# Two-block transformer stack on one core: at every norm the scaling of the rows goes ahead of the next weight splits on VectorE, and a bank wait on TensorE is narrowed

## The chip, the cores and the metric

The kernel runs on one core of a Trainium2 chip. The metric is the device time of one execution in microseconds. Line numbers are those of the kernel before.

## The reference

The input is one sequence of 256 rows of 1024 numbers in float32. Two parts follow one another. The first has two layers; each is a mixer (an mLSTM in layer 0, stick-breaking attention in layer 1), a cross-attention into 256 memory rows and a gated feed-forward of width 2816. Ahead of each stage the rows go through a root-mean-square norm, and what a stage gives is normed again and added:

```python
x = x + rms_norm(y, g[1])
y = memory_cross_attention(rms_norm(x, g[2]), mem_n, xa_w_q[layer], xa_w_kv[layer], xa_w_o[layer])
x = x + rms_norm(y, g[3])
y = swiglu_ffn(rms_norm(x, g[4]), ffn_w_gate_up[layer], ffn_w_down[layer])
x = x + rms_norm(y, g[5])
```

The second part has one layer: three mixers side by side (a gated recurrence, a forgetting attention, a memory attention), gated and merged, then a feed-forward with a short convolution. In all there are eight norms of the rows `xr` whose result goes into products, numbered 0 to 7.

## The kernel before, in words

Five engines run a program each and meet at semaphores. Each engine serves its own instructions in order, so the order in which a program is written decides what stands behind what.

**Weights.** All weights are streamed. They are cut into chunks in a fixed list (`order`), of which each has one or, mostly, two pieces of 128x1024 numbers. SyncE loads the chunks into `raw` (three buffers); it waits until the low halves of the chunk three back are made. Products are made in three terms so that they keep nearly float32 precision: each piece is split into a high half `whi`, which ScalarE makes (L989), and a low half `wlo = raw - whi`, which VectorE makes (L1468). Both have four buffers (`NSP`), and ScalarE waits for TensorE to have used the piece four back (`w_used`). `past(name)` on either engine makes all halves up to four pieces beyond the chunk `name`.

**Products.** `fm` (L373 to L375) multiplies a chunk piece by piece with the weights as the stationary operand, `tm` (L393 to L395) with the rows as the stationary operand, first both pieces for tile 0 (128 rows), then for tile 1. TensorE waits for each piece's low half (`w_lo`), and so for both its halves.

**A norm.** After a stage's last product ScalarE squares its result (`post_squares`, L1037), GpSimd makes the reciprocal root (`rstd`, L2034 and L2035), VectorE scales it and adds it to `xr` (`post_add`, L1516 and L1520); this is per tile. Then the next norm begins: ScalarE squares `xr` (`squares`, L1007), GpSimd makes the root, VectorE scales the rows (`normed`, L1488, semaphore `n_x`), TensorE transposes them (`norm_rows`, L418, 16 transposes), ScalarE makes the high half of each of the eight transposed rows blocks (`norm_hi`, L1021), VectorE the low half (`norm_lo`, L1498, semaphore `n_lo`), and products begin. At norm 7 `post_squares` is missing and the addition is a single instruction (`plain_add`, L1526).

TensorE has other work between a stage's last product and the transposes. At norm 1 these are the chunks K0_3 and V0_1a, at norm 2 K1_0 and K1_1, at norm 3 V1_0a and V1_0b, at norm 4 V1_1a and V1_1b, at norm 5 mka and mkb, at norm 6 mva and mvb, and at norm 7 nothing. Behind the transposes norm 1 has V0_1b and norm 2 has K1_2 ahead of the first product that uses the rows. At norm 4 VectorE also scales the memory rows (`mem_normed`) ahead of `norm_lo`.

The last stretch of the list of chunks ahead of norm 1 is mlw3, K0_3, V0_1a, V0_1b, xq0_0; ahead of norm 2 xo0_3, K1_0, K1_1, K1_2, then the feed-forward's g0_0, u0_0, g0_1; ahead of norm 7 mo3, g2_0, u2_0.

**The first feed-forward** puts its chunks g0_j in bank 4 or 6 and u0_j in bank 5 or 7, by turns: g0_0 in 4, u0_0 in 5, g0_1 in 6, u0_1 in 7. The keys chunk K1_2 ahead of it was multiplied into bank 6, and VectorE copies it out (`pair`, L1532, the fourth count of `K_dve`); K1_0 in bank 4 is the third. VectorE's program has the low halves of u0_0 ahead of that copy.

Of the kernel before, what the change touches and what calls it, by code (L numbers as in the profile page):

```python
# [19 lines left out]
NJ = FT // 2  # L20
# [62 lines left out]
def build_program(nc, I, out):  # L83
    ctx = ExitStack()
    with ctx:
# [67 lines left out]
        def gain2(r, n=8):  # L153
            return gcol[:, 96 + r:96 + r + n]
# [111 lines left out]
        def end(name):  # L266
            return C[name].end


        S = {}  # L270
# [87 lines left out]
        def half_bank(k, banks):  # L358

            return banks[k // 4 * 2 + k % 2], k % 4 // 2  # L360


        def tensor_program(pe):
            def fm(name, X, bank):

                for i, p in enumerate(C[name].pieces):
                    o = ps[:, bank, 256 * i:256 * i + 256]
                    pe.wait_ge(S["w_lo"], p.n + 1)
                    for k in range(8):
                        if X.met <= k:  # L370
                            pe.wait_ge(X.sem, X.need[k])
                            X.met = k + 1
                        pe.matmul(o, p.hi[:, k, :], X.h[:, k, :], start=k == 0, stop=False)  # L373
                        pe.matmul(o, p.hi[:, k, :], X.l[:, k, :], start=False, stop=False)  # L374
                        m = pe.matmul(o, p.lo[:, k, :], X.h[:, k, :], start=False, stop=k == 7)  # L375
                    m.then_inc(S["w_used"], 1)
# [55 lines left out]
            def keys(l, j, bank, M):  # L432
                fm(f"K{l}_{j}", M, bank)
# [70 lines left out]
            def feed_forward(f, X):  # L504
                act_done = "f_act" if f < 2 else "f_conv"

                def down(j):
                    e = NJ * f + j + 1
                    last = j == NJ - 1
                    pe.wait_ge(S["f_lo"], e)  # L510
                    h = Hr[j % 3]
                    pp = C[f"d{f}_{j}"].pieces
                    for i, t in ([(0, 0), (1, 0), (0, 1), (1, 1)] if last else [(0, 0), (0, 1), (1, 0), (1, 1)]):
                        p = pp[i]
                        if not t:
                            pe.wait_ge(S["w_lo"], p.n + 1)
                        r = slice(128 * t, 128 * t + 128)
                        for half in range(2):
                            o, c = ps[:, 2 * t + half, :], slice(512 * half, 512 * half + 512)
                            pe.matmul(o, h[:, i, r], p.hi[:, 0, c], start=j == 0 and i == 0, stop=False)  # L520
                            pe.matmul(o, h[:, i, r], p.lo[:, 0, c], start=False, stop=False)  # L521
                            m = pe.matmul(o, h[:, 2 + i, r], p.hi[:, 0, c], start=False, stop=last and i == 1)  # L522
                        if t:
                            m.then_inc(S["w_used"], 1)
                        elif last and i == 1:
                            m.then_inc(S["f_first"], 1)

                for j in range(NJ):
                    if j >= 2:
                        pe.wait_ge(S[act_done], NJ * (f if f < 2 else 0) + j - 1)  # L530
                    fm(f"g{f}_{j}", X, 4 + 2 * (j % 2))
                    if j >= 2:
                        pe.wait_ge(S["f_prod"], NJ * f + j - 1)
                    fm(f"u{f}_{j}", X, 5 + 2 * (j % 2))
                    if j >= 2:
                        down(j - 2)
                down(NJ - 2)
                down(NJ - 1)
# [97 lines left out]
            keys(1, 1, 5, M)  # L636
            X = norm_rows(2)
            keys(1, 2, 6, M)
            pe.wait_ge(S["K_dve"], 4)
            pe.wait_ge(S["K_act"], 3)  # L640
            feed_forward(0, X)


# [119 lines left out]
            pe.wait_ge(*at("mk_dve", 1))  # L763
            pe.wait_ge(*at("mk_act", 1))
            feed_forward(1, X)


# [691 lines left out]
        def vector_program(dve):  # L1459
# [3 lines left out]
            def lo_to(n):  # L1463

                while made[0] < min(n, len(pieces)):
                    p = pieces[made[0]]
                    dve.wait_ge(S["w_hi"], p.n + 1)
                    dve.tensor_tensor(p.lo, p.raw, p.hi.bitcast(F32), ALU.subtract).then_inc(S["w_lo"], 1)  # L1468
                    made[0] += 1

            def past(name):

                lo_to(end(name) + NSP)
# [6 lines left out]
            def gain_columns(i):  # L1480
                n, o, b = ((96, 0, 6), (53, 96, 6), (88, 149, 4))[i]
                dve.wait_ge(S["gains_T"], i + 1)
                dve.tensor_copy(gcol[:, o:o + n], ps[:, b, 0:n]).then_inc(S["gains"], 1)

            def normed(no):
                for t in range(NT):
                    dve.wait_ge(S["n_r"], 2 * no + t + 1)
                    dve.tensor_scalar(xn[:, t, :], xr[:, t, :], n_st[no][t][2], None, ALU.mult).then_inc(S["n_x"], 1)  # L1488

            def mem_normed(i):  # L1490
                for t in range(NT):
                    dve.wait_ge(S["m_r"], 2 * i + t + 1)
                    dve.tensor_scalar(mem_n[i][:, t, :], mem_tm[:, t, :], m_st[i][t][2], None, ALU.mult).then_inc(S["m_x"], 1)

            def rest(h, l, bank, half, g, sem, need, done):

                dve.wait_ge(*at(sem, need))
                dve.scalar_tensor_tensor(l, ps[:, bank, 256 * half:256 * half + 256], g, h.bitcast(F32), ALU.mult,  # L1498
                                         ALU.subtract).then_inc(S[done], 1)

            def norm_lo(no, g):
                for k in range(8):
                    b, half = half_bank(k, (0, 1, 2, 3))
                    rest(XTh[:, k, :], XTl[:, k, :], b, half, g[:, k:k + 1], "n_hi", 8 * no + k + 1, "n_lo")
# [7 lines left out]
            def post_add(i):  # L1512
                for t in range(NT):
                    dve.wait_ge(S["pa_sq"], 2 * i + t + 1)
                    dve.wait_ge(S[f"row_in{i}"], 16)
                    dve.tensor_tensor(heads(xn[:, t, :], 2), ps[:, 2 * t:2 * t + 2, :], heads(grow[:, i % 4, :], 2),  # L1516
                                      ALU.mult).then_inc(S["pa_m"], 1)
                    dve.wait_ge(S["pa_m"], 2 * i + t + 1)
                    dve.wait_ge(S["pa_r"], 2 * i + t + 1)
                    dve.scalar_tensor_tensor(xr[:, t, :], xn[:, t, :], pa_st[i][t][2], xr[:, t, :], ALU.mult,  # L1520
                                             ALU.add).then_inc(S["resid"], 1)
# [7 lines left out]
            def pair(dst, name, bank, sem):  # L1529

                dve.wait_ge(S["w_used"], end(name))
                dve.tensor_copy(dst, two(ps[:, bank, :])).then_inc(S[sem], 1)  # L1532

            def first_tile(dst, name, bank, sem):

                dve.wait_ge(S["tm_first"], C[name].tm_no)
                dve.tensor_copy(dst, ps[:, bank, :]).then_inc(S[sem], 1)
# [144 lines left out]
            first_tile(Vx[:, 0, 0:512], "V0_0b", 6, "V_dve")  # L1682
            past("mlw2")
            post_add(0)
            past("mlw3")


            normed(1)
            past("K0_3")
            past("V0_1a")  # L1690
            norm_lo(1, gain1(0, 2))
# [1 line left out]
            first_tile(Vx[:, 0, 512:1024], "V0_1b", 6, "V_dve")  # L1693
            cross_attention(0, {})
            post_add(1)
            past("xo0_3")


            normed(2)
            past("K1_0")  # L1700
            pair(Kx[:, 0:2, :], "K1_0", 4, "K_dve")
            past("K1_1")
# [2 lines left out]
            pair(Kx[:, 4:6, :], "K1_2", 6, "K_dve")  # L1705
            feed_forward(0)
            post_add(2)
            past(f"d0_{NJ - 1}")


            normed(3)
            past("V1_0a")
            first_tile(Vx[:, 0, 0:512], "V1_0b", 6, "V_dve")
            norm_lo(3, gain1(1, 0))
# [36 lines left out]
                    dve.tensor_tensor(Ol2[p], two(ps[:, 3, :]), Oh2[p].bitcast(F32), ALU.subtract).then_inc(S["sb_lo"], 1)  # L1751
            past("sbo2")
            post_add(3)
            past("sbo3")


            normed(4)
            gain_columns(2)
            mem_normed(1)
            past("V1_1a")  # L1760
# [2 lines left out]
            past("V1_1b")  # L1763
            cross_attention(1, {0: lambda: mem_lo(1, 0, gain2(24)), 1: lambda: mem_lo(1, 1, gain2(24))})
            post_add(4)
            past("xo1_3")


            normed(5)
            past("mka")  # L1770
            first_tile(mk[:, 0, :], "mkb", 6, "mk_dve")
            norm_lo(5, gain1(1, 4))
            past("mkb")
            feed_forward(1)
            post_add(5)
            past(f"d1_{NJ - 1}")


            normed(6)
            past("mva")  # L1780
            first_tile(mv[:, 0, :], "mvb", 6, "mv_dve")
            norm_lo(6, gain2(16))
# [3 lines left out]
            for h in range(4):  # L1786
                dve.wait_ge(S["h_f"], h // 2 + 1)
                f = dve.tensor_scalar(hf[:, h, :], hf[:, h, :], oml[:, h:h + 1], lb[:, h:h + 1], ALU.mult, ALU.add)
# [221 lines left out]
                rest(XTh[:, 4 + k, :], XTl[:, 4 + k, :], 4 + k, 0, 1.0, "mT_hi", 4 + k + 1, "mT_lo")  # L2010
            past("mo2")
            plain_add(("tm_first", C["mo3"].tm_no), ("w_used", end("mo3")))
            past("mo3")


            normed(7)
            norm_lo(7, gain2(32))
            feed_forward(2)
            plain_add(("f_first", 3), ("w_used", end(f"d2_{NJ - 1}")))
# [179 lines left out]
        @block.tensor  # L2199
        def _(e):  # L2200
            tensor_program(e)
# [25 lines left out]
```

## Time and profile before

| what | value |
|---|---|
| median of 3 runs | 1389.76 us (1388.7 to 1391.26) |
| the profiled execution's own time | 1391.61 us |
| its span | 1389.9 us |
| TensorE busy | 1346.4 us, 97% |
| VectorE busy | 787.9 us, 57% |
| ScalarE busy | 710.6 us, 51% |
| GpSimd busy | 106.4 us, 8% |
| mean granted clock of TensorE | 0.98 |

The profile is of one execution. In it PE is TensorE, PEld its weight load, DVE VectorE, ACT ScalarE, POOL GpSimd, SP SyncE. Times are microseconds from the start of the span. In a timeline a row has the start, the duration, the engine, the line, the operation, what it writes and reads, how many instructions are merged in it, and in brackets how long the engine had been idle and what released it. The granted clock is a share of full speed: 1.00 is 2.4 GHz and 0.50 is 1.2 GHz. Idle time of VectorE costs nothing unless TensorE ends up waiting for it.

### The profile page before, as it was taken

The page shows a single profiled execution, that of the slowest core. Times are in us where ns is not written, and L with a number is a line of the kernel's source. Part 1 is how long each engine was busy: PE and PEld are TensorE (multiplying, and loading weights), DVE is VectorE, ACT ScalarE, POOL GpSimd, SP SyncE. Part 2 cuts the span into 40 slices and gives each one's busy share as a digit, 9 for nine tenths or more (in the row PEclk, how much of TensorE's full clock was granted, in tenths as well). Part 3 has the DMA queues.
Part 4 walks back from the last instruction along what each step waited for, and adds up shares of the span by engine and source line. Part 5 has one row for each costly group of instructions (what it writes and reads, how often), then busy time and mean ns, then how long its engine had stood idle before and what let it go on. Part 6 is the DMA issues. An engine that isn't in the chain of part 4 may idle for free.

```text
span 1389.9 us, 19780 instructions
## 1 busy us (share of the span) xinstructions
PE 1346.4 (97%) x8409; PEld 1202.7 (87%) x8409; DVE 787.9 (57%) x924; ACT 710.6 (51%) x966; POOL 106.4 (8%) x173
## 2 busy tenths in 40 slices
PE   7999999999999999999999999999999999899998
PEld 6879898999998888779899999898776888799997
DVE  4456664655455644366564554657863566566665
ACT  4545544544444676755454444555544564455443
POOL 7000100100000100020100000101310002000000
PEclk9999999999999999999999999999988999999999
DMA  8644553555555543244365555543432444455552
GB/s 266 193 151 152 176 173 122 166 182 182 183 186 195 164 152 121 91 152 152 104 194 187 182 182 183 182 151 123 153 94 91 164 166 162 133 188 185 182 182 91
DMA packets 154793, 223.76 MB, mean 161 GB/s; under 512 B 6056, under 2 KB 106564, under 8 KB 154705
## 3 DMA queue, kind: packets, MB, share of 16 engines
q1 hardware_dynamic: 152912, 218.18, 47.9%
q0 software_dynamic: 1664, 4.27, 1.0%
q8 instruction: 66, 1.08, 0.3%
q14 instruction: 23, 0.18, 0.0%
q10 hardware_dynamic: 128, 0.05, 0.0%
HBM read 221.44 MB, written 1.05 MB: 160 GB/s over the span
## 4 chain that ended last, share of the span: by engine, by line
PE 87%; DVE 6%; ACT 4%; issue 1%; DMA 1%; POOL 0%; SPq 0%; DVEq 0%; ACTq 0%
PE ps L373 14%; PE ps L375 14%; PE ps L374 14%; PE ps L393 8%; PE ps L395 8%; PE ps L394 8%; PE ps L520 4%; PE ps L521 4%; PE ps L522 4%; DVE wlo L1468 2%; PE ps L418 2%; ACT whi L989 2%; PE ps L445 1%; PE ps L657 1%; PE ps L466 1%
## 5 line engine op out<-in xcount | busy, mean ns | idle before, releaser
L1468 DVE TENSOR_TENSOR wlo<-raw,whi 128x1024 fp32r<-128x1024 f32 x412 | 501.7, 1231 | 411.2 <-ACT whi L989 407.8
L989 ACT ACTIVATE whi<-raw 128x1024 fp32r<-128x1024 f32 x412 | 428.9, 1053 | 436.2 <-PE ps L375 269.3
L373 PE MATMUL ps<-RR,whi 128*128 128x256 f32 x1568 | 448.5, 286 | 13.4 <-DVE RR L1498 9.7
L375 PE MATMUL ps<-RR,wlo 128*128 128x256 f32 x1568 | 445.9, 284 | 0.0
L374 PE MATMUL ps<-RR,whi 128*128 128x256 f32 x1568 | 445.7, 284 | 0.0
L373 PEld LDWEIGHTS ps<-RR,whi 128*128 128x128 f32 x1568 | 303.2, 193 | 17.9 <-DVE RR L1498 10.8
L374 PEld LDWEIGHTS ps<-RR,whi 128*128 128x128 f32 x1568 | 303.2, 193 | 1.1
L375 PEld LDWEIGHTS ps<-RR,wlo 128*128 128x128 f32 x1568 | 302.9, 193 | 0.0
L393 PE MATMUL ps<-whi,RR 128*128 128x512 f32 x592 | 238.2, 402 | 0.9 <-DVE RR L1551 0.4
L395 PE MATMUL ps<-whi,RR 128*128 128x512 f32 x592 | 232.7, 393 | 0.0
L394 PE MATMUL ps<-wlo,RR 128*128 128x512 f32 x592 | 232.5, 393 | 0.0
L393 PEld LDWEIGHTS ps<-whi,RR 128*128 128x128 f32 x592 | 112.7, 190 | 27.4 <-issue 4.1
L395 PEld LDWEIGHTS ps<-whi,RR 128*128 128x128 f32 x592 | 112.3, 190 | 24.2
L394 PEld LDWEIGHTS ps<-wlo,RR 128*128 128x128 f32 x592 | 112.7, 190 | 22.3
L520 PE MATMUL ps<-whi,RR 128*128 128x512 f32 x264 | 103.0, 390 | 0.0
L521 PE MATMUL ps<-wlo,RR 128*128 128x512 f32 x264 | 103.0, 390 | 0.0
L522 PE MATMUL ps<-whi,RR 128*128 128x512 f32 x264 | 102.7, 389 | 0.0
L2034 POOL TENSOR_SCALAR st<-st 128x1 f32<-128x1 f32 (+2 forms) x44 | 18.5, 421 | 872.3 <-ACT xn L1037 726.8
L522 PEld LDWEIGHTS ps<-whi,RR 128*128 128x128 f32 x264 | 49.6, 188 | 10.5
L520 PEld LDWEIGHTS ps<-whi,RR 128*128 128x128 f32 x264 | 49.7, 188 | 9.6
L521 PEld LDWEIGHTS ps<-wlo,RR 128*128 128x128 f32 x264 | 49.7, 188 | 9.3
L1498 DVE SCALAR_TENSOR_TENSOR RR<-ps,gcol,RR 128x256 fp32r<-128x256 f32 x92 | 39.4, 478 | 14.0 <-ACT RR L1021 9.2
(309 smaller groups left out, 1054.9 us busy)
## 6 DMA issues: line engine op xcount, KB each, us to landing
raw<-in_ffn_w_gate_up SPq DMA_DIRECT2D x44, 1024.0 KB, 5.1
raw<-in_ffn_w_down SPq DMA_DIRECT2D x33, 1024.0 KB, 4.9
raw<-in_w_in SPq DMA_DIRECT2D x28, 1024.0 KB, 5.0
raw<-in_ffn_w_up SPq DMA_DIRECT2D x22, 1024.0 KB, 5.1
raw<-in_xa_w_kv SPq DMA_DIRECT2D x16, 1024.0 KB, 5.2
raw<-in_ml_w_in SPq DMA_DIRECT2D x12, 1024.0 KB, 5.4
raw<-in_sb_w_qkv SPq DMA_DIRECT2D x12, 1024.0 KB, 5.2
raw<-in_xa_w_q SPq DMA_DIRECT2D x8, 1024.0 KB, 5.2
```

The source lines that it names most:

```text
L373: pe.matmul(o, p.hi[:, k, :], X.h[:, k, :], start=k == 0, stop=False)
L374: pe.matmul(o, p.hi[:, k, :], X.l[:, k, :], start=False, stop=False)
L375: m = pe.matmul(o, p.lo[:, k, :], X.h[:, k, :], start=False, stop=k == 7)
L393: pe.matmul(o, X.h[:, g, r], p.hi[:, k, :], start=g == 0, stop=False)
L394: pe.matmul(o, X.h[:, g, r], p.lo[:, k, :], start=False, stop=False)
L395: m = pe.matmul(o, X.l[:, g, r], p.hi[:, k, :], start=False, stop=g == K - 1)
L520: pe.matmul(o, h[:, i, r], p.hi[:, 0, c], start=j == 0 and i == 0, stop=False)
L521: pe.matmul(o, h[:, i, r], p.lo[:, 0, c], start=False, stop=False)
L522: m = pe.matmul(o, h[:, 2 + i, r], p.hi[:, 0, c], start=False, stop=last and i == 1)
L989: act.activation(p.hi, p.raw, ACT.Copy).then_inc(S["w_hi"], 1)
L1468: dve.tensor_tensor(p.lo, p.raw, p.hi.bitcast(F32), ALU.subtract).then_inc(S["w_lo"], 1)
L1498: dve.scalar_tensor_tensor(l, ps[:, bank, 256 * half:256 * half + 256], g, h.bitcast(F32), ALU.mult, ALU.subtract).then_inc(S[done], 1)
```

## The change

At each of the norms 1 to 7, VectorE's call `normed(n)` moves ahead of the call of `past` that stood in front of it. Nothing else on VectorE changes its order, and ScalarE's order stays as it was. On TensorE the wait ahead of the first feed-forward asks for three copies of keys and no longer for four; the wait for the fourth stands ahead of its third chunk (g0_1).

```diff
                 for j in range(NJ):
+                    if f == 0 and j == 1:
+                        pe.wait_ge(S["K_dve"], 4)
                     if j >= 2:
...
             keys(1, 2, 6, M)
-            pe.wait_ge(S["K_dve"], 4)
+            pe.wait_ge(S["K_dve"], 3)
             pe.wait_ge(S["K_act"], 3)
             feed_forward(0, X)
...
             post_add(0)
+            normed(1)
             past("mlw3")
-            normed(1)
             past("K0_3")
...
             post_add(1)
+            normed(2)
             past("xo0_3")
-            normed(2)
             past("K1_0")
...
             post_add(2)
+            normed(3)
             past(f"d0_{NJ - 1}")
-            normed(3)
             past("V1_0a")
...
             post_add(3)
+            normed(4)
             past("sbo3")
-            normed(4)
             gain_columns(2)
...
             post_add(4)
+            normed(5)
             past("xo1_3")
-            normed(5)
             past("mka")
...
             post_add(5)
+            normed(6)
             past(f"d1_{NJ - 1}")
-            normed(6)
             past("mva")
...
             plain_add(("tm_first", C["mo3"].tm_no), ("w_used", end("mo3")))
+            normed(7)
             past("mo3")
-            normed(7)
             norm_lo(7, gain2(32))
```

## Rows read from the trace of the kernel before

**Rows 1.** Page, first table: busy time, share, instructions

```profile
PE 1346.4 (97%) x8409; PEld 1202.7 (87%) x8409; DVE 787.9 (57%) x924; ACT 710.6 (51%) x966; POOL 106.4 (8%) x173
```

**Rows 2.** Waits of TensorE: total us, times, longest us

```profile
PE ps L373 <- DVE RR L1498: 9.7, 5, 3.0
PE ps L418 <- DVE xn L1488: 9.2, 2, 6.5
```

**Rows 3.** Timeline of TensorE at norm 1

```profile
160.26 0.28 PE L373 MATMUL ps<-RR,whi 128*128 128x256 f32 x1
...
166.01 0.40 PE L393 MATMUL ps<-whi,RR 128*128 128x512 f32 x1
...
171.49 1.91 PE L418 MATMUL ps<-ident,xn 128*128 128x128 f32 x16
```

**Rows 4.** Timeline of VectorE at norm 1

```profile
164.07 2.35 DVE L1468 TENSOR_TENSOR wlo<-raw,whi 128x1024 fp32r<-128x1024 f32 x2
166.88 0.75 DVE L1488 TENSOR_SCALAR xn<-xr,st 128x1024 f32<-128x1024 f32 x1 [0.46 <-POOL st L2035]
168.35 0.75 DVE L1488 TENSOR_SCALAR xn<-xr,st 128x1024 f32<-128x1024 f32 x1 [0.71 <-POOL st L2035]
```

**Rows 5.** Timeline of ScalarE at norm 1, end of the second squares

```profile
165.36 0.18 ACT L1007 ACTIVATION_READ_ACCUMULATOR xn<-xr 128x1 f32 x1
```

**Rows 6.** Timeline of GpSimd at norm 1

```profile
165.42 1.43 POOL L2035 TENSOR_TENSOR st<-st,mhalf 128x1 f32<-128x1 f32 x1
166.93 0.75 POOL L2034 TENSOR_SCALAR st<-st 128x1 f32<-128x1 f32 x1
```

**Rows 7.** Timeline of GpSimd at norm 7, second tile

```profile
1190.01 0.19 POOL L2034 TENSOR_SCALAR st<-st 128x1 f32<-128x1 f32 x1 [1.89 <-ACT xn L1007]
1190.29 0.56 POOL L2035 TENSOR_TENSOR st<-st,mhalf 128x1 f32<-128x1 f32 x1
```

**Rows 8.** Timeline of VectorE, the moved pair at norms 2, 3 and 4

```profile
244.62 2.36 DVE L1468 TENSOR_TENSOR wlo<-raw,whi 128x1024 fp32r<-128x1024 f32 x2
...
455.12 2.35 DVE L1468 TENSOR_TENSOR wlo<-raw,whi 128x1024 fp32r<-128x1024 f32 x2
...
608.53 2.35 DVE L1468 TENSOR_TENSOR wlo<-raw,whi 128x1024 fp32r<-128x1024 f32 x2
```

**Rows 9.** Timeline of TensorE: transposes of norms 2, 3, 4, first product of norm 4

```profile
252.32 1.91 PE L418 MATMUL ps<-ident,xn 128*128 128x128 f32 x16
...
462.19 1.91 PE L418 MATMUL ps<-ident,xn 128*128 128x128 f32 x16
...
615.77 1.91 PE L418 MATMUL ps<-ident,xn 128*128 128x128 f32 x16
...
620.65 0.39 PE L373 MATMUL ps<-RR,whi 128*128 128x256 f32 x1 [2.98 <-DVE RR L1498]
```

**Rows 10.** Windows: stretch, its length, busy PE, PEld, DVE, ACT, POOL, PEclk, DMA

```profile
262.00:272.00 10.00, 9.02 (x63) 9.02 (x63) 2.55 (x4) 2.12 (x2) 0.00 (x0) 0.83 0.32 105
620.00:630.00 10.00, 9.35 (x66) 9.35 (x67) 6.84 (x10) 6.80 (x12) 0.00 (x0) 0.83 0.62 200
456.00:470.00 14.00, 12.38 (x80) 10.99 (x79) 10.86 (x17) 8.97 (x16) 3.10 (x4) 1.00 0.48 151
```

**Rows 11.** Page, DMA issues: KB each, us to landing

```profile
raw<-in_xa_w_kv SPq DMA_DIRECT2D x16, 1024.0 KB, 5.2
```

**Rows 12.** Timeline of TensorE, start of the first feed-forward

```profile
262.99 0.38 PE L373 MATMUL ps<-RR,whi 128*128 128x256 f32 x1 [3.01 <-DVE Kx L1532]
```

**Rows 13.** Timeline of VectorE at norm 7

```profile
1187.53 1.22 DVE L1526 TENSOR_TENSOR xr<-xr,ps 128x1024 f32<-128x1024 f32 x1 [1.50 <-PE ps L395]
1190.90 2.36 DVE L1468 TENSOR_TENSOR wlo<-raw,whi 128x1024 fp32r<-128x1024 f32 x2 [2.16 <-ACT whi L989]
...
1197.14 0.88 DVE L1498 SCALAR_TENSOR_TENSOR RR<-ps,gcol,RR 128x256 fp32r<-128x256 f32 x2 [2.55 <-ACT RR L1021]
```

**Rows 14.** Timeline of TensorE at norm 7

```profile
1193.98 3.68 PE L418 MATMUL ps<-ident,xn 128*128 128x128 f32 x16 [6.50 <-DVE xn L1488]
1197.77 0.55 PE L373 MATMUL ps<-RR,whi 128*128 128x256 f32 x1
```

## The prediction

> **What bounds the kernel now.** The page's first table comes first: TensorE is busy for 97% of the span [rows 1], so a change counts only by what it adds to or takes from TensorE's idle time, or by the clock at which it runs. VectorE is busy 57%, but its queue is served in order, so what matters there is when an instruction comes up. Next the list of TensorE's waits: on the split rows of a norm (L1498) it waits 9.7 us in five places, and on the scaled rows (L1488) only twice, 9.2 us together [rows 2]. One of these two is the start, which the change leaves alone; the other is the norm of the last feed-forward, 6.50 us [rows 14]. So at the other six norms TensorE never waits for what the change brings forward. Then, norm by norm, I put the timelines of TensorE, VectorE, ScalarE and GpSimd side by side.
>
> **What TensorE does meanwhile.** `past(name)` makes low halves up to four pieces beyond the chunk named, so at each norm the moved call makes exactly two pieces, those of one chunk: V0_1a, K1_1, V1_0b, V1_1b, mkb, mvb and, at norm 7, u2_0. In `tensor_program`, norms 1 to 6 have two chunks queued between the last product and their transposes, and the moved pieces are the second of them (at norm 2, K1_1 after K1_0). So TensorE comes to them one chunk, 5.5 to 5.75 us, after the block has ended, while the norm is still running. At norm 1 it takes K0_3 at 160.26 and V0_1a at 166.01, without a gap, and the transposes at 171.49 [rows 3].
>
> **Before, at norm 1.** VectorE makes the two low halves from 164.07, 2.35 us for both [rows 4]; the first is there at about 165.3, only 0.7 us before TensorE takes it. They lie where VectorE would otherwise wait for the squares and the root, so they are nearly free. Behind the change they stand behind the scaling of both tiles, which cannot start before the second tile's root.
>
> **The moved halves, step by step.** The second squares end at 165.36 + 0.18 = 165.54 [rows 5]. GpSimd's first instruction starts 0.1 us behind and is slowed by the scaling of tile 0: where the two meet before the change, it takes 0.75 us [rows 6]; as the scaling will have begun a little before, I take 0.63. The power takes 0.56 us beside an idle VectorE [rows 7]. With 0.1 us between them, the root is there 1.4 us after the squares; the scaling of tile 1 takes 0.75 [rows 4] and the first low half 1.2, with 0.05 to TensorE: 3.3 us behind the squares, 168.85 to 168.9. TensorE wanted it at 166.01, so it stalls 2.9 us. The second half is wanted 1.4 us after the first and comes 1.15 after, so it costs nothing.
>
> The other norms run by the same clockwork: the pair of low halves starts 1.47 us before the squares end (164.07 and 165.54 at norm 1). Hence each new first half comes 1.47 + 3.3 = 4.8 us after the start of the present pair, and TensorE wants it one chunk ahead of its transposes. Norm 2: 244.62 + 4.8 = 249.4 against 252.32 - 5.75 = 246.57, a stall of 2.9. Norm 3: 455.12 + 4.8 = 459.9 against 462.19 - 5.48 = 456.7, 3.2. Norm 4: 608.53 + 4.8 = 613.3 against 615.77 - 5.48 = 610.3, 3.0 [rows 8, 9]. Norms 5 and 6 repeat norm 3 to 0.01 us in the distance from the pair to the transposes (7.08 us), so 3.2 each. The chunk lengths are those of norm 1: 5.75 us for one of keys (160.26 to 166.01), 5.48 for one of values (166.01 to 171.49). **Six stalls: 2.9 + 2.9 + 3.2 + 3.0 + 3.2 + 3.2 = 18.4 us.**
>
> What is given back: at norms 1 to 3, 5 and 6 nothing. Transposes and split rows follow the stalled chunk and shift with it; at norms 3 and 6 the 1.6 us wait on the split rows depends on transposes, ScalarE's half and VectorE's half, and VectorE is idle before them. At norm 4 TensorE waits 2.98 us there [rows 9], since VectorE is still busy with the scaling of the memory rows; when TensorE comes 3.0 later, that shortens to the 1.6 us of norm 3 (14.00 less 12.38 us busy, [rows 10]). **Minus 1.3 us.**
>
> Other queues: the loads on SyncE wait for low halves, so one load per norm is issued some 3.6 us later. It fills the chunk three ahead, over 10 us of TensorE's work away; a load takes about 5 us from issue to landing [rows 11]. I cost it at nothing; without that cover each would add at most those 3.6 us. GpSimd loses nothing: its roots run freer, because the halves no longer lie beside them.
>
> **The clock.** After the 3.01 us stall at the first feed-forward the granted clock averages 0.83 over the 10 us that follow: part of them is at 1.2 GHz, and 10 x 0.17 = 1.7 us of work is lost. The same 0.83 stands behind norm 4's 2.98 us. Norm 3's stall of 1.6 us leaves it at 1.00 [rows 10]. The new stalls are as long as the two that cost clock. Bounds for five new ones (norm 4's loss only moves ahead): 0 and 5 x 1.7 = 8.5; I take four, **6.8 us**, because two out of two is all there is.
>
> **The first feed-forward.** TensorE waits 3.01 us for the copy of bank 6 [rows 12]. Its first two chunks use banks 4 and 5, and the copy is over long before the third, 11 us on. The chunk's pieces are made ahead of that copy, so nothing takes over. The wait goes, and so does the clock lost behind it: **3.0 + 1.7 = 4.7 us gained.**
>
> **Norm 7.** Nothing lies between block and transposes. The second root is there at 1190.29 + 0.56 = 1190.85 [rows 7], but the pair of low halves runs from 1190.90 to 1193.26 ahead of both scalings [rows 13]. With the change tile 0 is scaled from 1187.53 + 1.22 = 1188.75, when the addition is over, tile 1 at 1190.9 to 1191.65. The pair then ends at 1194.0, beside the transposes. TensorE's first product comes 0.63 us after the first split row starts (1197.14 and 1197.77, [rows 13, 14]), so at 1194.6 in place of 1197.77: 3.2 us gained. The halves now lie ahead of the split rows; without them there it would be more. The gaps around the transposes still leave room for a low clock over the first products, at up to 1.7 us; I take **2.4 us**, between 1.5 and 3.2.
>
> **Sum.** 18.4 - 1.3 + 6.8 - 4.7 - 2.4 = +16.8 us. The profiled execution took 1391.61 us for a span of 1389.9, 1.85 above the median of 1389.76; what lies around the span doesn't change. So the profiled one would take 1408.4, and a median of **1406.6 us**, 1.2% slower.
>
> A rule on GpSimd. Beside the low halves of norm 1 the power took 1.42 us, at norm 7 0.56 [rows 6, 7]. The Trainium skill, GPSIMD Engine Reference, section 8 (Key points), says that GpSimd shares its SBUF interfaces with VectorE and collides with VectorE instructions that have two SBUF inputs, as the low half has. By that rule the freed power takes 0.56 us and the sum stays +16.8; if the 1.42 stood, each of six stalls would be 0.86 us longer, +22.0.
>
> **The rivals.** (A) The cover holds and the kernel gets faster. It needs the moved halves to be wanted 3.6 us later than I read. Then no stall comes, and 4.7 + 3.2 = 7.9 us are gained: 1381.9. The point at which it decides is the slack at V0_1a: 0.7 us by [rows 3, 4], and 3.6 are needed. Only a misread order on TensorE would save it. 6 in 100. (B) The stalls come, the clock doesn't fall behind them: 18.4 - 1.3 - 1.7 - 4.7 - 3.2 = +7.5, 1397.3. For it: no stall of before lay inside a stream like this. 12 in 100. (C) GpSimd's root stays slow, as beside the present halves: 0.86 x 6 = 5.2 more, 1411.8. Against it: VectorE will be waiting then. 8 in 100. (D) The first feed-forward stalls for something else, say the split rows that come later after norm 2's stall: 4.7 more, 1411.3. But the wait there ends with the copy [rows 12], the rows were there before, and both shift together. 4 in 100. (E) Stalls and gains cancel within 0.2% (2.8 us): it would need stalls of 1 us and no clock lost. 4 in 100. The forecast has 66.
>
> **Numbers.** 1406.6 us. Low end: B, 1397. High end: five clock losses and norm 7 at 1.5, which is +19.4, with half of C's 5.2: 1412. A measurement of this kernel tells about 0.2% (three runs spread over 2.6 us) from no change. Faster 0.06, same 0.04, slower 0.90.
>
> **What would show it.** TensorE's waits get a new entry, on the low halves L1468, six times about 3 us, at K1_1 on L373 and otherwise on L393. The entry on the copy of the first feed-forward is gone. The wait on L1488 falls from 6.5 to some 2 us plus a short one. The granted clock is under 0.9 over the 10 us behind at least four of the new stalls. The prediction is wrong if VectorE's second scaling ends over 1 us earlier than 2.1 us after the squares, if the halves' first reader is later than the chunk given, or if the clock holds.

## The result, and the profile after

The changed kernel takes 1405.09 us in the median of four runs (1403.64 to 1407.34), against 1389.81 for the kernel before (1388.7 to 1391.26): ratio 1.0112, 95% interval 1.0097 to 1.0127. It is slower by 15.3 us, where 16.8 were forecast. The profiled execution has a span of 1402.8 us, 12.9 more than that of before; this is the difference that can be followed row by row. It is smaller than 15.3 mainly because the profiled execution of before took 1.85 us more than its median. Lines behind the two new ones on TensorE are two further down than before: L1470 is the low half, L1490 the scaling, L1500 the split rows, L2037 GpSimd's power.

The page's first table of the changed kernel: TensorE's work is the same, its share smaller, and GpSimd is busy 8 us less.

```profile
PE 1349.5 (96%) x8409; PEld 1203.3 (86%) x8409; DVE 787.9 (56%) x924; ACT 710.1 (51%) x966; POOL 98.3 (7%) x173
```

TensorE's waits in the changed kernel (total us, times, longest). Against [rows 2], two entries on the low halves are new, five waits on L393 and one on L373; the entry on the bank copy, 3.0 us before [rows 12], is gone; the wait on scaled rows has fallen.

```profile
PE ps L393 <- DVE wlo L1470: 14.6, 5, 3.0
PE ps L373 <- DVE RR L1500: 8.8, 6, 2.5
PE ps L418 <- DVE xn L1490: 5.9, 3, 2.8
...
PE ps L373 <- DVE wlo L1470: 2.7, 1, 2.7
```

The timeline of VectorE at norm 1 in the changed kernel, which answers to [rows 4]. The scaling of tile 0 starts at 165.41 where the halves used to run, the second waits for its root until 166.88, and only then come the halves, four in a row.

```profile
165.41 0.75 DVE L1490 TENSOR_SCALAR xn<-xr,st 128x1024 f32<-128x1024 f32 x1 [1.31 <-POOL st L2037]
166.88 0.75 DVE L1490 TENSOR_SCALAR xn<-xr,st 128x1024 f32<-128x1024 f32 x1 [0.71 <-POOL st L2037]
167.55 4.63 DVE L1470 TENSOR_TENSOR wlo<-raw,whi 128x1024 fp32r<-128x1024 f32 x4
```

The timeline of GpSimd in the same place, which answers to [rows 6]. Both powers take 0.56 us now; the first took 1.43 beside the low halves. The multiply that meets the scaling still takes 0.64, which is why the second root is only 1.47 us earlier.

```profile
164.82 0.56 POOL L2037 TENSOR_TENSOR st<-st,mhalf 128x1 f32<-128x1 f32 x1
165.58 0.64 POOL L2036 TENSOR_SCALAR st<-st 128x1 f32<-128x1 f32 x1 [0.20 <-ACT xn L1009]
166.30 0.55 POOL L2037 TENSOR_TENSOR st<-st,mhalf 128x1 f32<-128x1 f32 x1
```

The timeline of TensorE in the changed kernel: the six stalls in order of the norms, the transposes of norm 1, the waits on split rows at norms 3, 4 and 6, and norm 7. Each row with brackets is the first product after the idle time in brackets.

```profile
168.92 0.77 PE L393 MATMUL ps<-whi,RR 128*128 128x512 f32 x1 [2.80 <-DVE wlo L1470]
176.03 1.91 PE L418 MATMUL ps<-ident,xn 128*128 128x128 f32 x16
...
253.97 0.46 PE L373 MATMUL ps<-RR,whi 128*128 128x256 f32 x1 [2.70 <-DVE wlo L1470]
...
464.15 0.50 PE L393 MATMUL ps<-whi,RR 128*128 128x512 f32 x1 [3.00 <-DVE wlo L1470]
...
473.28 0.39 PE L373 MATMUL ps<-RR,whi 128*128 128x256 f32 x1 [1.63 <-DVE RR L1500]
...
620.88 0.50 PE L393 MATMUL ps<-whi,RR 128*128 128x512 f32 x1 [2.85 <-DVE wlo L1470]
...
629.99 0.39 PE L373 MATMUL ps<-RR,whi 128*128 128x256 f32 x1 [1.62 <-DVE RR L1500]
...
702.53 0.50 PE L393 MATMUL ps<-whi,RR 128*128 128x512 f32 x1 [3.00 <-DVE wlo L1470]
...
906.83 0.79 PE L393 MATMUL ps<-whi,RR 128*128 128x512 f32 x1 [3.00 <-DVE wlo L1470]
...
918.76 0.39 PE L373 MATMUL ps<-RR,whi 128*128 128x256 f32 x1 [1.62 <-DVE RR L1500]
...
1205.07 1.09 PE L418 MATMUL ps<-ident,xn 128*128 128x128 f32 x8 [1.98 <-DVE xn L1490]
1207.30 1.97 PE L418 MATMUL ps<-ident,xn 128*128 128x128 f32 x8 [1.13 <-DVE xn L1490]
1210.05 0.55 PE L373 MATMUL ps<-RR,whi 128*128 128x256 f32 x1 [0.79 <-DVE RR L1500]
```

The reader is to see four things. The six stalls add to 17.35 us. The wait on the split rows at norm 4 has shrunk from 2.98 us [rows 9] to 1.62, that of norm 3 has not shrunk. The first product of a norm can be laid beside that of before: norm 4's is at 629.99 for 620.65, a shift of 9.3 us; norm 7's at 1210.05 for 1197.77 [rows 14], 12.3 us. And at norm 7 the 6.50 us in one piece have become 1.98 and 1.13 and 0.79.

The windows of the changed kernel, 12 us that begin one to two us before the end of each stall (length, busy PE, PEld, DVE, ACT, POOL, then PEclk, the mean granted clock). A stretch in which the clock is at 1.2 GHz is called a low stretch from here on. The clock is at 1.00 behind norms 3, 4 and 5; behind norms 1 and 2 it is 0.86, which is 12 x 0.14 = 1.7 us of work lost, and behind norm 6 0.72, 3.4 us.

```profile
167.00:179.00 12.00, 10.08 (x46) 8.46 (x47) 8.07 (x9) 3.83 (x6) 0.00 (x0) 0.86 0.53 175
252.00:264.00 12.00, 10.03 (x72) 10.03 (x73) 8.51 (x9) 3.88 (x6) 0.00 (x0) 0.86 0.55 175
463.00:475.00 12.00, 9.22 (x54) 7.95 (x55) 8.03 (x12) 3.92 (x10) 0.00 (x0) 1.00 0.55 176
619.00:631.00 12.00, 8.49 (x48) 7.25 (x49) 9.83 (x15) 6.52 (x14) 3.60 (x4) 1.00 0.53 175
701.00:713.00 12.00, 9.80 (x56) 8.37 (x57) 8.04 (x13) 3.68 (x10) 0.00 (x0) 1.00 0.56 176
905.00:917.00 12.00, 10.17 (x40) 8.29 (x40) 5.87 (x6) 1.38 (x4) 0.00 (x0) 0.72 0.56 175
```

### The profile page after: what moved, and what is told of

Same layout as the page of the kernel before. It is cut to its first block, busy times and chain, and to the rows that moved or that the text cites. A ratio compares the mean times of both kernels' runs of the same rounds, so it can differ in the third digit from the quotient of the medians.

```text
span 1402.8 us, 19781 instructions
## 1 busy us (share of the span) xinstructions
PE 1349.5 (96%) x8409; PEld 1203.3 (86%) x8409; DVE 787.9 (56%) x924; ACT 710.1 (51%) x966; POOL 98.3 (7%) x173
## 3 DMA queue, kind: packets, MB, share of 16 engines
HBM read 221.44 MB, written 1.05 MB: 159 GB/s over the span
## 4 chain that ended last, share of the span: by engine, by line
PE 85%; DVE 7%; ACT 5%; issue 2%; POOL 1%; DMA 1%; SPq 0%; POOLq 0%; DVEq 0%; ACTq 0%
PE ps L373 13%; PE ps L374 13%; PE ps L375 13%; PE ps L393 8%; PE ps L394 8%; PE ps L395 8%; PE ps L521 4%; PE ps L520 4%; PE ps L522 4%; DVE wlo L1470 2%; ACT whi L991 2%; PE ps L418 1%; PE ps L445 1%; ACT xn L1009 1%; PE ps L659 1%
## 5 line engine op out<-in xcount | busy, mean ns | idle before, releaser
L1470 DVE TENSOR_TENSOR wlo<-raw,whi 128x1024 fp32r<-128x1024 f32 x412 | 501.2, 1231 | 409.3 <-ACT whi L991 405.9
L373 PE MATMUL ps<-RR,whi 128*128 128x256 f32 x1568 | 448.1, 286 | 12.0 <-DVE RR L1500 8.8
L373 PEld LDWEIGHTS ps<-RR,whi 128*128 128x128 f32 x1568 | 302.8, 193 | 16.5 <-DVE RR L1500 9.0
L393 PE MATMUL ps<-whi,RR 128*128 128x512 f32 x592 | 240.4, 406 | 15.6 <-DVE wlo L1470 14.6
L393 PEld LDWEIGHTS ps<-whi,RR 128*128 128x128 f32 x592 | 113.5, 192 | 44.2 <-DVE wlo L1470 13.5
L394 PEld LDWEIGHTS ps<-wlo,RR 128*128 128x128 f32 x592 | 113.6, 192 | 22.4
L2036 POOL TENSOR_SCALAR st<-st 128x1 f32<-128x1 f32 (+2 forms) x44 | 14.6, 332 | 890.1 <-ACT xn L1039 743.5
L1500 DVE SCALAR_TENSOR_TENSOR RR<-ps,gcol,RR 128x256 fp32r<-128x256 f32 x92 | 39.4, 478 | 20.9 <-ACT RR L1023 16.1
```

The lines of the kernel that those rows point to most:

```text
L393: pe.matmul(o, X.h[:, g, r], p.hi[:, k, :], start=g == 0, stop=False)
L394: pe.matmul(o, X.h[:, g, r], p.lo[:, k, :], start=False, stop=False)
```

## The experiments

The kernel before ran beside each of them on the same chip. Its medians there were 1389.59 us (the first four), 1390.22 (the next four) and 1389.69 (the last four). Three theories were to be told apart: the stalls come from the first low half being late for TensorE (the prediction); something else that the order brings slows TensorE; the bank wait or norm 7 has a part in the loss.

**1. The bank wait alone.**

```diff
                 for j in range(NJ):
+                    if f == 0 and j == 1:
+                        pe.wait_ge(S["K_dve"], 4)
...
-            pe.wait_ge(S["K_dve"], 4)
+            pe.wait_ge(S["K_dve"], 3)
```

> The kernel before with the narrowed bank wait alone. Theory (the wait is a true stall and the low clock behind it is its cost): TensorE's 3.01 us wait on the copy of bank 6 goes with no successor, and the granted clock over the 10 us behind it returns to 1.00, so -3.0 to -4.7 us, some 1385 to 1387 us. Rival (the first feed-forward then waits for something else there): within 1 us of before.

Measured: 1385.21 us, ratio 0.9969 (0.9958 to 0.998), 4.4 us faster. The 3.01 us wait is gone without a successor. The interval, 2.8 to 5.8 us, holds the wait alone (3.0) as well as the wait and a low stretch behind it (4.7). The window at the start of the feed-forward has TensorE busy throughout at the full clock:

```profile
259.00:271.00 12.00, 12.00 (x103) 12.00 (x102) 6.38 (x7) 5.47 (x6) 0.00 (x0) 1.00 0.45 144
```

**2. Norm 7 alone.**

```diff
             plain_add(("tm_first", C["mo3"].tm_no), ("w_used", end("mo3")))
+            normed(7)
             past("mo3")
-            normed(7)
```

> The kernel before with only norm 7's scaling ahead of the halves. Theory: the first product of the last feed-forward starts 3.2 us earlier, part of it is lost again to the low clock, -2.4 us (1.5 to 3.2), some 1387.4 us. Rival (the two halves, now ahead of the split rows, take the gain back): 0, 1389.8 us.

Measured: 1386.67 us, ratio 0.9981 (0.9973 to 0.999), 2.9 us faster. Its first product stands at 1194.54, 3.23 us before that of [rows 14], the waits ahead of it being the same 1.98, 1.13 and 0.79 as in the changed kernel.

**3. Norms 1 to 6 alone.** The six swaps of the change, the bank wait and norm 7 as before.

> The kernel before with the scaling ahead of the halves at norms 1 to 6, the bank wait and norm 7 as before. Theory: six stalls on the low halves of 2.7 to 3.0 us, together 17.4, less 1.4 at norm 4, and one to four low-clock stretches at 1.7 us each: +18 to +23 us, some 1408 to 1413 us. Rival (part of the whole change's loss comes from the new bank wait or from norm 7): under +15.

Measured: 1417.23 us, ratio 1.0194 (1.0181 to 1.0208), 27.6 us slower, beyond the 18 to 23 expected. All the loss of the change is here, and more. The waits are those of the changed kernel to 0.01 us (its list has 14.6 and 2.7 us on the low halves), so the stalls can't be what was expected too low. The clock was: up to four low stretches of 1.7 us had been expected. Its windows behind norms 3, 5 and 6, and behind the 3.01 us bank wait:

```profile
469.00:481.00 12.00, 10.04 (x40) 8.23 (x40) 5.98 (x6) 1.44 (x3) 0.00 (x0) 0.72 0.56 175
...
711.00:723.00 12.00, 9.88 (x46) 8.13 (x46) 6.83 (x10) 2.44 (x7) 0.00 (x0) 0.86 0.55 175
917.00:929.00 12.00, 9.08 (x53) 7.82 (x54) 8.03 (x13) 3.78 (x9) 0.00 (x0) 1.00 0.56 177
```

```profile
272.00:284.00 12.00, 11.07 (x70) 11.07 (x71) 3.32 (x4) 2.12 (x2) 0.00 (x0) 0.72 0.27 87
```

Norm 3, which cost no clock in the changed kernel, costs 3.4 us here, norm 5 1.7, norm 6 nothing where it cost 3.4, and the bank wait 3.4 where it cost 1.7 in the kernel before. Five of the six stalls have a low stretch behind them, 10.2 us of work in all, against 6.8 in the changed kernel.

**4. Bank wait and norm 7 together, norms 1 to 6 as before.** The edits of 1 and 2.

> The kernel before with the bank wait and norm 7, norms 1 to 6 as before. Theory (the parts are independent): the sum of the two single runs, -5.5 to -7.5 us, some 1382 to 1384 us, and TensorE has no wait on a weight half. Rival (they share a cause or one hides the other): no more than the better of the two alone.

Measured: 1384.38 us, ratio 0.996 (0.9947 to 0.9973), 5.2 us faster, just short of the 5.5 to 7.5 expected, for 7.3 by the sum of 1 and 2. Its interval is 3.8 to 7.4 us: it can't be told from that sum, nor from the 4.4 of run 1 alone. That both parts are there is read from its profile: no wait on the bank copy, and 1.98 and 1.13 us ahead of norm 7's transposes in place of 6.50.

**5. One half ahead.** The changed kernel, but at each of norms 1 to 6 the first of the two moved halves stays ahead of the scaling. For norm 1:

```diff
             post_add(0)
+            lo_to(end("mlw3") + NSP - 1)
             normed(1)
             past("mlw3")
```

> The changed kernel, but at norms 1 to 6 the first of the two low halves stays ahead of the scaling and only the second comes behind it. Theory (each stall is TensorE's wait for the first half that is late): at norms 1, 3, 4, 5 and 6 the stall moves to the second half, which is wanted 1.36 us later, and shrinks to about 2 us; at norm 2 the second is wanted 2.9 us later and the stall falls under 0.6. Stalls 11 us in all, and at most two low-clock stretches: +0.7 to +5 us against the kernel before, 1390 to 1395 us. Rival (TensorE is slowed by something else that the order brings, such as the later loads or GpSimd): the loss stays above +10.

Measured: 1398.72 us, ratio 1.0058 (1.0044 to 1.0071), 8.5 us slower than before. The stalls did what the theory says. The timeline of its TensorE at norms 1 and 2:

```profile
170.20 0.50 PE L393 MATMUL ps<-whi,RR 128*128 128x512 f32 x1 [1.87 <-DVE wlo L1470]
...
252.93 0.39 PE L373 MATMUL ps<-RR,whi 128*128 128x256 f32 x1 [0.38 <-DVE wlo L1470]
```

Together the six are 10.6 us (17.35 in the changed kernel), and at norm 2, where the second piece is wanted latest, 0.38 are left of 2.70. The total missed the 0.7 to 5 us given, but also the rival's +10. The windows say why in part: stalls of 1.94 to 2.19 us at norms 3, 5 and 6 were still followed by a low clock, those of 1.87 at norm 1 and 2.04 at norm 4 were not. The third low stretch takes the upper end of what was expected from 5 to 6.7 us, and its span is 1396.6, 6.7 above the first profile of before; that profile's execution was 1.85 us above its median, which leaves 8.5 by the medians. Its windows behind norms 3 and 4:

```profile
458.00:470.00 12.00, 9.32 (x47) 7.82 (x48) 6.75 (x11) 3.79 (x9) 0.00 (x0) 0.86 0.55 176
615.00:627.00 12.00, 8.49 (x53) 7.46 (x54) 9.78 (x16) 7.38 (x14) 3.46 (x4) 1.00 0.52 175
```

**6. Norm 3 alone.** The swap around `past(f"d0_{NJ - 1}")` in the kernel before.

> The kernel before with only norm 3's scaling ahead of the halves. Theory: one stall of 3.0 us at V1_0b, nothing given back by the 1.6 us wait on the split rows behind it: +3.0 us if the clock holds there, as it did at this norm in the changed kernel, +4.7 if it falls. Rival (the later wait on the split rows absorbs part of the stall): +1.4 or less.

Measured: 1393.01 us, ratio 1.0019 (1.001 to 1.0028), 2.8 us slower. One stall of 3.00 us, and the wait on the split rows behind it stays at 1.62. Nothing is absorbed: the interval, 1.4 to 3.9 us, only touches the rival's 1.4, and the wait behind hasn't shrunk. In its profile the clock behind that stall is 0.86; behind the same stall it was 1.00 in the changed kernel and 0.72 in run 3.

**7. The memory rows late.** Run 4, and at norm 4 the scaling of the memory rows behind the split rows:

```diff
             gain_columns(2)
-            mem_normed(1)
             past("V1_1a")
             first_tile(Vx[:, 0, 512:1024], "V1_1b", 6, "V_dve")
             norm_lo(4, gain1(1, 2))
+            mem_normed(1)
```

> Bank wait and norm 7 as in the change, norms 1 to 6 as before, and at norm 4 the scaling of the memory rows behind the low halves of the split rows. Theory (at norm 4 TensorE waits 2.98 us because VectorE is still at the memory rows, and 1.6 us would be left without them): the wait falls to 1.6 us, and the low clock behind it goes: -1.4 to -3.1 us against the run with bank wait and norm 7 alone, some 1379.5 to 1382 us. Rival (the transposes of the memory rows behind the first query chunk then wait as long): no difference to that run.

Measured: 1379.01 us, ratio 0.9915 (0.9899 to 0.9931), 5.4 us under run 4, more than expected. The first product of norm 4 in its timeline:

```profile
613.30 0.39 PE L373 MATMUL ps<-RR,whi 128*128 128x256 f32 x1 [1.62 <-DVE RR L1500]
```

The 1.6 us are as given (run 4 waits 3.23 there), and the low clock behind is gone. In its profile a low stretch behind a 2.16 us wait ahead of norm 4, at L669, is missing too, with that wait unchanged; this accounts for another 1.7 in the profile. That part isn't the move's: run 9 has the move without it and gains 2.9 us.

**8. Norm 7's halves last.** Run 7, and `past("mo3")` behind `norm_lo(7, ...)`.

```diff
             normed(7)
-            past("mo3")
             norm_lo(7, gain2(32))
+            past("mo3")
```

> As the run with the memory rows late, and at norm 7 the two low halves behind the split rows too. Theory: VectorE takes up the split rows as soon as ScalarE has the first, the 0.79 us wait behind the transposes goes, and the halves of u2_0 are wanted only a chunk later: -0.5 to -0.8 us more. Rival (the halves are then late for u2_0, or the transposes at the low clock set the start anyway): 0 or slower.

Measured: 1378.08 us, ratio 0.9911 (0.9898 to 0.9925). The step over run 7 is 0.9 us by the medians and can't be told from nothing by the intervals. The wait on the split rows is gone: TensorE's first product follows the transposes at once, 4.31 us after the first of them (1178.34); in run 7 it came after 4.99 us (1178.96 to 1183.95). So the profiles have the product 0.7 us earlier.

```profile
1180.57 1.97 PE L418 MATMUL ps<-ident,xn 128*128 128x128 f32 x8 [1.13 <-DVE xn L1490]
1182.65 0.55 PE L373 MATMUL ps<-RR,whi 128*128 128x256 f32 x1
```

**9. The memory rows late, alone.** The edit of run 7 in the kernel before.

> The kernel before with only the scaling of the memory rows moved behind the split rows at norm 4. Theory: TensorE's wait there falls from 3.0 to 1.6 us, too short to bring the low clock, so -1.4 to -3.1 us, some 1387 to 1388.5 us. Rival (the run with bank wait, norm 7 and memory rows gained 5.4 us over the one without the memory rows, so the move itself is worth over 4): -5 us.

Measured: 1386.78 us, ratio 0.9977 (0.9968 to 0.9987), 2.9 us faster: the theory's, not the rival's.

**10, 11 and 12. The changed kernel twice more, the kernel before once more.** One execution each, for its profile.

> The changed kernel once more, for a second profile. Theory (whether and how long the clock falls behind a stall of 2.7 to 3.0 us depends on when the stall lies, not on the kernel): the seven waits repeat to 0.1 us, while the low-clock stretches behind the six stalls, which in the first profile lay behind norms 1, 2 and 6 and not behind 3, 4 and 5, fall elsewhere. Rival (the place decides: what TensorE runs around the stall): they lie behind norms 1, 2 and 6 again.

> The changed kernel a third time, for a third profile. Theory and rival as in the second: under the theory the pattern of low-clock stretches behind the six stalls differs again, under the rival it is the same three places.

> The kernel before once more, for a second profile. Theory: the waits of 3.0 us at the first feed-forward and at norm 4 repeat, and the low-clock stretch behind them may be longer, shorter or missing. Rival (the place decides): 3.4 us of low clock behind each of the two, as in the first profile.

Measured: 1402.41, 1405.26 and 1388.61 us. In 10 and 11 the six stalls repeat to 0.01 us. At norm 7 the wait on the split rows is 1.66 us in both, where the first profile has 0.79; the first product still comes 4.98 us after the first transpose in all three. In run 12 the wait at norm 4 is 3.23 us, not 2.98. The windows of run 10 behind norms 1, 4 and 6:

```profile
167.00:179.00 12.00, 10.10 (x53) 8.58 (x54) 9.41 (x12) 5.34 (x10) 0.00 (x0) 1.00 0.59 187
...
617.00:629.00 12.00, 9.20 (x41) 7.49 (x42) 8.25 (x12) 5.26 (x11) 3.24 (x4) 0.86 0.53 175
...
904.00:916.00 12.00, 8.82 (x40) 7.20 (x40) 7.01 (x9) 2.62 (x7) 0.00 (x0) 0.86 0.56 175
```

And the window of run 12, the kernel before, behind its bank wait, where the first profile had 0.83 over ten us [rows 10]. Of the six profiles with this wait of 3.0 us, that of before and those of runs 2 and 3 have a low stretch behind it, those of runs 6, 9 and 12 have none:

```profile
263.00:275.00 12.00, 10.59 (x88) 10.59 (x89) 4.30 (x5) 3.18 (x3) 0.00 (x0) 1.00 0.35 108
```

Behind norm 1 the clock fell in the first profile and in neither of the others; behind norm 4 in both others and not in the first; behind norm 6 it fell over a double, a single and a double length. Norm 2 always had one, norms 3 and 5 never, in this kernel; in run 3 both did. So the rival, that the place decides, is refuted by norms 1 and 4 and by the bank wait of before. The theory's strong form, that nothing but the moment matters, isn't shown: norms 2, 3 and 5 repeated. Runs 10 and 11 agree with each other in every place and differ only in length. What in the moment decides wasn't tried.

## Why the prediction was right, step by step

**The stalls.** Forecast 2.9, 2.9, 3.2, 3.0, 3.2, 3.2, together 18.4 us; measured 2.80, 2.70, 3.00, 2.85, 3.00, 3.00, together 17.35, or some 18 from start to start. The idle time starts at the end of the last product, 0.1 us after the next could have started; from start to start, norm 1's chunk V0_1a moved from 166.01 to 168.92, the 2.9 us of the forecast. VectorE's second scaling ends 2.1 us after the squares, as forecast (165.49 and 167.63). Shown by run 3 (they and the clock behind them make the loss), run 6 (one alone makes its own) and run 5 (the stall follows the half that is late and shrinks with the cover: 0.38 us left at norm 2).

**What norm 4 gives back.** Forecast 1.3, measured 2.98 - 1.62 = 1.36 (1.6 against the 3.23 of run 12). Norm 3 gives nothing back, in the change and in run 6.

**The bank wait.** Forecast 4.7, of it 1.7 for the clock. Run 1: 4.4, in an interval of 2.8 to 5.8. The wait's 3.0 are shown; the 1.7 for the clock holds in the first profile of before, but three of six profiles with this wait have no low stretch behind it, so as a gain of the median it isn't shown. Rival D, another wait in its place, is refuted by run 1.

**Norm 7.** Forecast 3.2 us at the first product and 2.4 in the end. In the changed kernel the first product's shift falls from 15.61 us (the end of the block, 1205.07 - 1.98 against 1193.98 - 6.50) to 12.28, a gain of 3.3, and 0.6 are lost by the end of the span (12.9). Run 2: 2.9.

**The clock.** Forecast 6.8 us net: low stretches of 1.7 us behind four of the five new stalls, with norm 4's old one only moved ahead. In the first profile the low stretches behind the six stalls are 1.7 + 1.7 + 3.4 = 6.8 us, behind three stalls; norm 4 has none, so its old 1.7 comes off, and 5.1 are added. The forecast was 1.7 us too high, wrong in its reason (each stall as long as those two costs clock), and wrong in the sign it gave to look for (below 0.9 behind at least four stalls). "Two out of two is all there is" took a chance for a rule. The three profiles of the changed kernel give three of six stalls each, 6.8, 5.1 and 6.8 us, and run 3 five of six, 10.2. Rival B, no clock lost at all, is refuted by each of them, and so is C: the power takes 0.56 us (beside the low halves it had taken 1.43 by its row, for the 1.42 of the forecast). A and E fall with the stalls.

**The loads.** Priced at nothing. The only wait of TensorE on a load in the changed kernel is the one at the start, 4.6 us, where before has 4.7. This agrees.

**The sum by the profile.** The terms as measured are 17.35 - 1.36 + 6.8 - 1.7 (norm 4's old low stretch) - 3.0 - 1.7 (bank wait and its low stretch) - 2.7 (norm 7, 3.3 - 0.6) = +13.7 us, where the forecast summed to 16.8: stalls 1.05 and clock 1.7 too high, norm 7's gain 0.3 too small. The span grew by 12.9. Between TensorE's wait of 1.8 us that ends at 987.89 before and at 1005.14 in the changed kernel (17.25 later) and the end of the last block (15.61 later) the changed kernel won 1.6 us that no edit explains; its low stretches there are 3.4 us shorter in all, worth 1.7 us of work. Without this the span would have grown by 14.5. The 0.8 us above 13.7 are about what the idle times leave out at the six stalls, 0.1 us each.

That the median moved by 15.3, closer to 16.8 than the profile did, is partly luck. The prediction rested on a profile of before whose execution lay 1.85 us above its median, with a low stretch behind the bank wait, for one, that run 12 doesn't have. Against run 12 (span 1386.9) the three profiles of the changed kernel (1402.8, 1400.7, 1403.5) are 15.9, 13.8 and 16.6 us longer.

**Why parts don't add up.** Norms 1 to 6 alone +27.6, bank wait and norm 7 -5.2; together +15.3, not +22.4. The stalls of run 3 and of the changed kernel are equal. By their profiles run 3 loses 10.2 us against 6.8 behind them, waits 3.0 us for the bank, loses 3.4 behind that, and lacks norm 7's 2.7: 3.4 + 3.0 + 3.4 + 2.7 = 12.5 us, for 12.1 by the medians (1417.23 - 1405.09) and 12.9 by the spans. Not in this sum are 1.0 us ahead of norm 1 (its stall ends at 169.95 for 168.92), the low stretch at L667 that run 3 lacks (-1.7), and 3.4 us more in low stretches after 1000 us (+1.7); with them it is 13.5. Why run 3 is hit so often stays open; its lowest timed run is 1415.38, so it isn't its profile alone.

## What to carry to other kernels

When an instruction is brought forward in an in-order queue, price what it passes: find the first reader of each passed result and its slack. Here some 0.4 to 0.7 us of slack stood against some 3.5 us of delay, six times, while the result brought forward had a reader that wasn't waiting in six of seven places. Take the swap only where the reader waits (norm 7), and look at the row behind a wait for what VectorE is busy with (the memory rows): with these and the bank wait the kernel takes 1378.08 us, 0.9911 (0.9898 to 0.9925) of the kernel before.

## What the runs showed of the hardware

A stall of TensorE of 1.9 to 3.0 us inside a full stream was followed by the 1.2 GHz level in part of the cases: at three of six stalls in each profile of the changed kernel, at five of six in run 3, at three of the five of 1.87 to 2.19 us in run 5, and the same stall at norm 3 was followed by 1.00, 0.86 and 0.72 over 12 us in three kernels, which is 0, 1.7 and 3.4 us of work. The waits of 1.6 us on split rows, at norms 3 and 6 before and at 3, 4 and 6 in the changed kernel, were not followed by it. The same kernel's profiled spans lay between 1400.7 and 1403.5 us, those of before at 1389.9 and 1386.9. So a comparison of single profiles can be off by some us, and the low stretches that differ between them are large enough to make that up.

A small GpSimd operation (the power, 128x1) took 1.43 us beside VectorE's low halves and 0.56 us when they had moved (norm 1, the timelines of GpSimd before and after).
